# A block of seven products: its 1 MB of weights in one transfer instead of two halves

## What is computed

```python
def swiglu(x, w_in, w_out):
    a, b = jnp.split(x @ w_in, 2, axis=-1)      # w_in 1024 x 5632, a and b 2816 columns each
    return (jax.nn.silu(a) * b) @ w_out
```

## Time and profile before

| | |
|---|---|
| median of 3 runs | 879.09 us (878.91 to 879.40) |
| the profiled execution, its time | 879.82 us |
| its span in the trace | 878.0 us |
| TensorE busy | 866.2 us, 99% of the span |
| VectorE, ScalarE, GpSimd busy | 59%, 41%, 10% |
| granted TensorE clock | 0.999 of full speed |
| DMA | 90.36 MB, mean 103 GB/s |
| upper and lower halves of the blocks | 18 + 18 transfers of 512 KB, issued from 549.95 to 729.95 us |

### The profile page before, as it was taken

One profiled execution on the slowest core, in us unless ns is written; L12 is line 12 of the kernel. 1 busy time (PEld: TensorE's weight loads), 2 busy tenths in 40 slices (PEclk: granted clock), 3 DMA queues, 4 the chain that ended last, 5 costly groups with the idle time before them and its releaser, 6 DMA issues.

```text
span 878.0 us, 13249 instructions
## 1 busy us (share of the span) xinstructions
PE 866.2 (99%) x5167; PEld 752.0 (86%) x5167; DVE 514.7 (59%) x962; ACT 359.6 (41%) x721; POOL 83.9 (10%) x103
## 2 busy tenths in 40 slices
PE   8999999999999999999999999999999999999996
PEld 8988898877678888888889879899999999888885
DVE  4344347768632626252767589498888888422354
ACT  4112156239642232323335544356665656311221
POOL 3100000081210000000000010111111121000000
PEclk9999999999999999999999999999999999999999
DMA  8535530430003333336423211223233332522211
GB/s 287 164 96 132 132 97 25 144 97 2 1 12 98 100 97 99 97 105 236 163 96 116 77 49 49 97 97 96 98 96 98 123 117 97 184 100 99 102 68 72
DMA packets 70808, 90.36 MB, mean 103 GB/s; under 512 B 3149, under 2 KB 62359, under 8 KB 70751
## 3 DMA queue, kind: packets, MB, share of 16 engines
q1 hardware_dynamic: 70367, 89.15, 31.2%
q0 software_dynamic: 384, 0.43, 0.3%
HBM read 87.05 MB, written 2.52 MB: 102 GB/s over the span
## 4 chain that ended last, share of the span: by engine, by line
PE 95%; DVE 2%; issue 1%; DMA 1%; ACT 1%; SPq 0%; DVEq 0%; POOLq 0%; POOL 0%; ACTq 0%
PE ps L2122 21%; PE ps L2123 21%; PE ps L2124 21%; PE ps L2691 7%; PE ps L2693 7%; PE ps L2692 7%; PE ps L2287 3%; PE ps L2364 3%; PE ps L2324 2%; PE ps L2159 1%; DMA x_nat<-in_x 1%; PE ps L2749 1%; PE ps L2750 1%; PE ps L2751 1%; PE ps L2636 0%
## 5 line engine op out<-in xcount | busy, mean ns | idle before, releaser
L2122 PE MATMUL ps<-xt_hi,w_hi 128*128 128x512 f32 (+1 forms) x400 | 155.6, 389 | 0.3 <-DVE w_lo L1957 0.3
L2124 PE MATMUL ps<-xt_lo,w_hi 128*128 128x512 f32 (+1 forms) x400 | 154.8, 387 | 0.0
L2123 PE MATMUL ps<-xt_hi,w_lo 128*128 128x512 f32 (+1 forms) x400 | 154.8, 387 | 0.0
L1036 ACT CAST w_hi<-raw 128x1024 fp32r<-128x1024 f32 (+1 forms) x57 | 58.9, 1037 | 170.6 <-PE ps L2124 162.1
L1440 DVE TENSOR_TENSOR w_lo<-raw,w_hi 128x1024 fp32r<-128x1024 f32 (+1 forms) x57 | 68.6, 1205 | 90.6 <-ACT w_hi L1036 90.3
L1749 DVE TENSOR_TENSOR w_lo<-raw,w_hi 128x1024 fp32r<-128x1024 f32 x30 | 36.7, 1224 | 90.1 <-ACT w_hi L1203 90.1
L2122 PEld LDWEIGHTS ps<-xt_hi,w_hi 128*128 128x128 f32 x400 | 75.1, 188 | 16.2 <-issue 1.1
L2124 PEld LDWEIGHTS ps<-xt_lo,w_hi 128*128 128x128 f32 x400 | 75.1, 188 | 15.4
L2123 PEld LDWEIGHTS ps<-xt_hi,w_lo 128*128 128x128 f32 x400 | 75.1, 188 | 15.0
L2691 PE MATMUL ps<-xt_hi,w_hi 128*128 128x256 f32 x288 | 81.6, 283 | 0.6 <-ACT ht L1335 0.6
L2692 PE MATMUL ps<-xt_hi,w_lo 128*128 128x256 f32 x288 | 81.5, 283 | 0.0
(11 more groups left out here) (346 smaller groups left out, 1852.5 us busy)
## 6 DMA issues: line engine op xcount, KB each, us to landing
raw<-in_w_in SPq DMA_DIRECT2D x24, 1024.0 KB, 5.0
raw<-in_w_ffn_in SPq DMA_DIRECT2D x36, 512.0 KB, 4.4
raw<-in_w_ffn_out SPq DMA_DIRECT2D x11, 1024.0 KB, 4.8
raw<-in_w_mix_out SPq DMA_DIRECT2D x4, 1024.0 KB, 4.8
raw<-in_w_ffn_in SPq DMA_DIRECT2D x4, 1024.0 KB, 5.2
raw<-in_w_branch_b SPq DMA_DIRECT2D x4, 512.0 KB, 4.0
resid<-in_x SPq DMA_DIRECT2D x1, 2048.0 KB, 9.4
raw<-in_w_xkv SPq DMA_DIRECT2D x2, 1024.0 KB, 5.3
```

The lines of the kernel that those rows point to most:

```text
L1036: act.copy(hi, src).then_inc(hi_done, 1)
L2122: pe.matmul(dst, a_hi, b_hi, start=start, stop=False)
L2123: pe.matmul(dst, a_lo, b_hi, start=False, stop=False)
L2124: return pe.matmul(dst, a_hi, b_lo, start=False, stop=stop)
```

## The change

The two transfers of a block become one of 1 MB that is counted by raw_in. The semaphores half_in go. t1 on GpSimd and the cast for P1 on ScalarE, which waited for the upper half, now wait for the whole piece, with the count of raw_in that t2, P2 and P3 wait for. Nothing else changes; the order of all instructions on TensorE, VectorE, ScalarE and GpSimd is as before, and SyncE issues 18 transfers fewer.

```diff
@@ semaphores
-        half_in = [sem(f"half_in{i}") for i in range(2)]
@@ SyncE, in the loop over n of N_BLOCK
                     sp.wait_ge(op_lo, PRODUCT["P3", n - 2] + 1)
                 k8 = raw[q][:, :].rearrange("p (k c) -> p k c", k=KT)
                 n0 = (N_WHOLE + n // 2) * 256 + q * D_FF
-                sp.dma_start(k8[:, 0:4, :], w_f1[:, 0:4, n0:n0 + 256]).then_inc(half_in[q], 16)
-                sp.dma_start(k8[:, 4:8, :], w_f1[:, 4:8, n0:n0 + 256]).then_inc(raw_in[q], 16)
+                sp.dma_start(k8, w_f1[:, :, n0:n0 + 256]).then_inc(raw_in[q], 16)
@@ GpSimd, weight_sums(n)
-                pool.wait_ge(half_in[n % 2], 16 * (1 + n // 2))
+                pool.wait_ge(raw_in[n % 2], F_IN[n % 2] + 16 * (N_WHOLE + 1 + n // 2))
@@ ScalarE, op_round(kind, n)
                 if kind == "P1":
-                    act.wait_ge(half_in[n % 2], 16 * (1 + n // 2))
+                    act.wait_ge(raw_in[n % 2], F_IN[n % 2] + 16 * (N_WHOLE + 1 + n // 2))
```

## The result

| | before | after |
|---|---|---|
| median of 20 runs each | 879.27 us | 881.21 us |
| ratio | | 1.0021, 95% interval 1.0014 to 1.0027 |
| span of the profiled execution | 878.0 us | 879.5 us |
| first matmul of P1(0), last of P3(17) | 567.88, 750.91 | 566.90, 752.39 |
| from the one to the other | 183.03 us | 185.49 us |

The change costs 1.9 us by the medians (1.2 to 2.4 us by the interval). The forecast was 2.2 us and 881.3. One of the 20 runs of the changed kernel took 1738.9 us, which no trace explains; the ratio leaves it out, and without it the median is 0.02 us lower. The spans differ by 1.5 us only, because the profiled execution of before lost more in its first 60 us, a part the change does not touch: TensorE is busy 57.49 us there before and 58.42 after, by the busy time of that stretch in the two traces.

What follows compares the result with a forecast made beforehand. TensorE was taken as the bound, nearly without a gap. Stalls 0.65 (block 2) + 0.9 (block 9) + 0.5 (block 12) + 0.2 (block 10) - 0.05 = 2.2 us took the median from 879.09 to 881.3; range 879.4 to 883.2.

Steps and rivals of the forecast that it cites:

- Bound: Stretch of the blocks: TensorE busy 180.60 of 181.00 us; the change costs only where an operand comes late.
- The faster rival: VectorE gets ahead and TensorE's gaps close: 878.7 us at best; chance 0.03 together with no change.
- Landing: Load of a block: the 1 MB transfer lands 5.1 us after its issue, against +3.5 for the upper half before.
- The lo of P1 at L + 1.9: VectorE, each block: held by t1, the lo of P1 is ready 1.9 us after landing L, +7.0 for L = 5.1.
- Block 2: Before P1(2): operand wanted at +6.42, ready at +7.0 to +7.1; stall with restart 0.65 us.
- Block 9: Late landing at 6.8 us: P4(8) ready at +10.5, wanted at +9.65; stall 0.9 us, up to 1.3.
- Block 12: Late landing at 6.3 us: lo of P1 ready at +8.2, wanted at +7.78; stall 0.5 us.
- Block 10: After block 9 VectorE runs late: P1 wanted at +7.1, ready at +7.0, P4(10) close as well; 0.2 us.
- Which blocks: Late loads: blocks 9 and 12, slow before with an instruction transfer beside them, were expected to be hit again.
- t4: VectorE: t4, no longer held by t1, takes 0.69 us again, freeing 1.1 us that is worth nothing on the path.
- Rival, a stall in every second block: Blocks from 2 on: transfer of 5.4 us or more, or t1 of 1.8 us; 884 us or above; chance 0.13.
- Rival, nearly all hidden: Landing at 4.9 to 5.0: only block 2 and at most one late block stall; +0.8, 879.9 us; chance 0.29.

Runs made afterwards that it cites:

- the early upper half: Kernel before, upper half's load issued as soon as its buffer half is free: ratio 1.0012 from block 2 on, 0.9998 from block 3 on.
- The short t1: Changed kernel, t1 from block 1 on computed for 2 of 128 columns of each row tile only: ratio 1.0003 to the kernel before.
- the run with t1 twice: Changed kernel with t1 computed twice in succession on GpSimd: ratio 1.0193, 17.2 us over the kernel before.
- the shifted instructions: Changed kernel plus 64 TensorE waits for counts long reached, just ahead of the blocks, shifting its instruction transfers: ratio 1.0028 to the kernel before.

## Why the prediction was right

- **Bound.** TensorE's clockwork with gaps only where an operand is late: as read. The faster rival had nothing to stand on, and the early upper half shows it from the other side.
- **Landing.** 5.0 us for 5.1 taken.
- **The lo of P1 at L + 1.9.** Right: block 2 at L = 4.9 had it at +6.86, block 12 at L = 6.1 at +8.01, block 9 at L = 6.3 at +8.18. The short t1 shows that this term, not the form of the transfer and not the cast, makes most of the loss. The sum holds where VectorE is free as soon as the cast is done; in six other blocks VectorE came to the lo of P1 later and t1 held it for less.
- **Block 2.** 0.59 us for 0.65.
- **Block 9.** 0.50 us for 0.9. The mechanism was right: the lo of P4(8) was what ended last (0.37 us, after 0.13 before P1(9)). But L was 6.3, not 6.8: the term was mis-sized in the landing, taken from one late pair of halves.
- **Block 12.** 0.40 us for 0.5.
- **Block 10.** Nothing for 0.2. Its P1 was wanted at +7.2 and ready at +6.79, as its load landed at +4.9; forecast were +7.1 and +7.0.
- **Which blocks.** Here the step failed. "I expect the same blocks to be hit" held for 9 and 12, but blocks 6 and 15 lost 0.51 and 0.53 us as well, as large as the two that I had counted. "Two blocks have slow transfers" was a misreading: in the trace of before the lower half of block 6 landed at +5.6 too, with an instruction transfer 0.9 us after the issue (t1 at +4.30, which a half could afford and a whole cannot), and I left it out. Block 15 is hit in some executions only; its instruction transfer fell 0.5 us before the issue in the trace of before. That the sum still came out (2.2 forecast, 2.46 in the trace, 1.9 by the medians) is partly the luck of errors of both signs: 0.4 too much in block 9, 0.2 in block 10, 0.2 in blocks 2 and 12, and 1.0 too little in 6 and 15.
- **t4.** "Today t1 mostly meets t4(n-1)" is right, but t4 was the one that waited in 8 of 18 blocks only, so the 1.1 us that the prediction gives back to VectorE were there in those alone. They were counted as worth nothing, and the sum does not change.
- **Rival, a stall in every second block.** Not so: eleven of the fifteen blocks from 3 on have no gap. But the run with t1 twice shows how near it was: 0.5 to 0.9 us of VectorE's time in a block were left.
- **Rival, nearly all hidden.** Falls with the gaps in five blocks. The fit of the Trainium skill (DMA: Bandwidth & Descriptors, anatomy of one DMA), by which 1 MB would take 4.4 us and all would be hidden, did not hold here; 18 transfers took 4.8 us at least. The section gives that fit for transfers issued from GpSimd, and the page's rule on two halves speaks of halves of the partitions; these loads are issued from SyncE, and their halves are row tiles of all 128 partitions. The prediction mentions neither difference.

## What to carry to other kernels

Before merging two transfers, look at who starts on the first one. Here the first half fed an operation on GpSimd, and moving that by 1.5 us put it on top of a VectorE operation with less room, though no engine's total grew. Read the room of each operand against its consumer block by block, with the latest landing of the trace and not the median one; and count the time that GpSimd keeps VectorE out as VectorE's own.

## What was not expected of the hardware

- VectorE and GpSimd were known to exclude each other from the trace of before. New is how little was left: 9.2 us of 10.08 in a block were taken by the trace, 9.6 by the sum, so that another 1.3 us of GpSimd work in each block cost 17 us. Which of the two waits changes from block to block: before the change t4 took 1.78 us in 8 blocks of 18, and t1 1.5 to 1.9 us in 16.
- A 16 KB instruction transfer that started within 3.1 us after the issue of a 1 MB load went with a landing 0.2 to 1.5 us later than the usual 5.0, in 18 of 18 cases. One that started up to 0.6 us before the issue mostly did no harm: with the shifted instructions block 6 (0.35 us before) landed at +4.8, but block 9 (0.04 before) at +6.0. Landings as late as +7.1 for the second of two halves occurred too.
- The first 60 us of the profiled executions differ by up to 0.9 us in TensorE's busy time (57.49 to 58.42) between executions of kernels that are the same there. Here this made the spans differ by 1.5 us where the blocks differ by 2.5: a difference of this size says little without the stage it comes from.
